# Storing the sample attention's mask and decays once, and repeating their rows while loading

## The chip, the core and the metric

One core of a Trainium2 chip runs the whole program. The metric is the device time of one execution, in microseconds; the time before is the median of three executions. Everything is float32. The engines named below are TensorE (PE in the profile, PEld its weight loads), VectorE (DVE), ScalarE (ACT), GpSimd (POOL) and SyncE (SP). SP, ACT and POOL issue DMA transfers, which the core's 16 DMA engines carry.

## What is computed

The reference is one inference step of a two-layer encoder trunk for two request groups with shared weights: a prompt group (1 x 256 tokens) and a sample group (8 requests x 16 new tokens, each with 512 cached keys, so 528 keys). A layer is SwiGLU, a token mixer, and SwiGLU again. The mixer has three attention branches of 6 heads x 64. What matters here is what is added to the scores of the sample group in two of them:

```python
def forgetting_attention(q, k, v, g_q, g_k, q_pos, k_pos):      # branch B
    s = einsum('bqhd,bkhd->bhqk', q, k) * scale
    s = s + g_kt[:, :, None, :] - g_q...        # decay: one row of keys per request and HEAD, the same for all tokens
    p = softmax(where(mask, s, -inf))

def dsa_attention(...):                          # branch C
    isc = ...                                    # indexer score per request, TOKEN and key, the same for all heads
    vals, idx = top_k(isc, topk)                 # the kernel keeps all keys and adds a mask of 0 or -1e30
    s = einsum(q, k_sel) * scale
    p = softmax(where(valid, s, -inf))
```

So the decays are 8 x 6 = 48 distinct rows of 528 numbers (g, without the query's own term, which a softmax does not need), and the mask is 8 x 16 = 128 distinct rows of 528.

## The kernel before, in words

The program is written out by hand, engine by engine, with semaphores; every engine runs its list in order. All work is in one function, `program`, with one block for each engine.

The sample attention of a layer runs in 18 steps (`NSTEP`), six for each branch: steps 0 to 5 stick-breaking, 6 to 11 forgetting, 12 to 17 DSA. A step (`UNIT = 4`) takes four pairs of heads: 4 pairs x 2 heads x 16 tokens fill the 128 partitions. Its scores are made by L1187 on PE into two banks; then L2328 on DVE scales them and adds the bias tile `BX[s % 2]`; DVE takes the maxima (L2341), ACT the exponentials (L1632), PE turns the probabilities one step later (L1158 and, for the new keys, L1164), multiplies them with the values (L1178), and forms the output two steps later (L1147). L2290 on DVE copies that output away, and stands behind L2328 in the DVE's list; L1164 on PE waits for it. PE also turns the keys of step s + 2 within step s (L1113). Eleven of the steps carry half a gate tile more (L1138); of steps 10 to 15 these are 11, 13 and 15.

Keys, values and bias stream from DRAM during the steps. `load_keys` (L572, SP) brings 768 KB for each request and branch into one of three buffers, as soon as PE has turned the keys that stood there. `load_values` and `load_new_values` (L1700, L1706, POOL) do so for the values with four buffers. `load_bias` (L1718, POOL) brings the bias of step s + 2 when L2328 of step s has read its buffer; there are two, `BX[0]` and `BX[1]`, both in the tile `MASKS`.

The bias comes from two scratch tensors in DRAM, `scr_g_sample` (`g_s`) and `scr_mask_sample` (`m_s`), each with a row for every request, head and token (768 x 528), so that a step's 128 rows lie in one piece. They are filled by SP:

- decays: `GX` (48 rows, in the tile QR) goes to `g_s` by one DMA (L539) that reads each row 16 times. This is during the projections, long before the steps.
- mask: DVE chooses the keys, in rounds between its other work, and ends in step 9 (`max(ROUND_S)`) with L2350, which writes the 128 rows of `WKS` (in the tile RING) as 0 or -1e30. SP then issues eight DMAs (L587), one for each request, each of which reads 16 rows 6 times. POOL waits for all eight (`msk_stored`) at the head of its step 10, and only then issues the bias of step 12, the first that reads `m_s`; the value loads of the DSA branch stand behind that wait in its list. On SP the remaining key loads of the DSA branch stand behind the eight stores.

Of the kernel before, what the change touches and what calls it, by code (L numbers as in the profile page):

```python
# [18 lines left out]
F32 = mybir.dt.float32  # L19

P = 128
# [3 lines left out]
NB = 8  # L25
NT = 16
# [5 lines left out]
KEYS = PAST + NT  # L32
PC = PAST // P
NH = 6
# [4 lines left out]
SB, FOX, DSA = range(NBR)  # L39
# [69 lines left out]
UNIT = 4  # L109
NU = NB * NPAIR // UNIT  # L110
# [27 lines left out]
def program(nc, t):  # L138
    with ExitStack() as ctx:
# [92 lines left out]
        WKS = RING[:, 7168 + MIX:7168 + MIX + KEYS]  # L232
# [40 lines left out]

        PS = ctx.enter_context(nc.psum_tensor("PS", [P, 8, 512], F32))

        g_s = nc.dram_tensor("scr_g_sample", (NB * NH * NT, KEYS), F32, kind="Internal").ap()
        g_p = nc.dram_tensor("scr_g_prompt", (NH, NPROMPT), F32, kind="Internal").ap()
        m_s = nc.dram_tensor("scr_mask_sample", (NB * NH * NT, KEYS), F32, kind="Internal").ap()


        def sems(name):
# [87 lines left out]
        def _(sp):  # L369
# [126 lines left out]
            for l in range(DEPTH):  # L496
# [5 lines left out]
                for i in range(N_PROJ):  # L502
# [33 lines left out]
                    if i == 9:  # L536
                        sp.wait_ge(g_ready, l * 2 + 2)
                        sp.dma_start(g_p, RSTD[0:NH, 0:NPROMPT]).then_inc(g_stored, 16)
                        sp.dma_start(g_s.rearrange("(g t) k -> g t k", t=NT),  # L539
                                     GX[0:48, :][:, None, :].to_broadcast([48, NT, KEYS])).then_inc(gs_stored, 16)  # L540

                def gates(g):
                    r = R_GATE + g - 1
# [34 lines left out]
                for s in range(-2, NSTEP):  # L578
                    for n in range(KBUF, NCACHE):
                        if last_unit(n - KBUF)[0] == s + 2:  # L580
                            load_keys(n)
                    if s == -1:
                        gates(7)
                    if s == max(ROUND_S):
                        sp.wait_ge(msk_ready, l * 3 + 3)
                        for b in range(NB):
                            sp.dma_start(m_s[b * NH * NT:(b + 1) * NH * NT, :].rearrange("(h t) k -> t h k", t=NT),  # L587
                                         WKS[b * NT:(b + 1) * NT, :][:, None, :].to_broadcast([NT, NH, KEYS])).then_inc(msk_stored, 16)

                w = t["w_branch"][l].rearrange("n (k p) d -> p (n k) d", p=P)  # L590
                for i in range(N_BRANCH):
                    r = R_BRANCH + i
                    if i < 2:
                        sp.wait_ge(gate_ready, l * 24 + 21 + 3 * i)
                        sp.wait_ge(msk_stored, (l + 1) * NB * 16)
                    else:
                        sp.wait_ge(br_ready, l * 24 + 6 * (i - 1))
                    load(l, r, by_k(l, r, w, i * 256, 256, k=9))
# [1095 lines left out]
        def _(pool):  # L1694
            for l in range(DEPTH):
# [12 lines left out]
                def load_bias(s):  # L1708

                    if s < NU + 2:  # L1710
                        pool.wait_ge(zs_ready, l * NSTEP + s + 1)
                    else:
                        pool.wait_ge(bx_free, l * 2 * NU + s - NU - 1)
                    if s == NU + 1:
                        pool.wait_ge(ps_ready, (l + 1) * NU)
                    settle(pool)
                    rows = (g_s, m_s)[s // NU - FOX]
                    pool.dma_start(BX[s % 2], rows[s % NU * P:(s % NU + 1) * P, :]).then_inc(bx_full[s % 2], 16)  # L1718

                pool.wait_ge(p_done, l * 6 + 2)  # L1720
                load_values(0)
# [8 lines left out]
                    load_new_values(n)  # L1730
                for s in range(NSTEP):
                    if s + 2 == 2 * NU:
                        pool.wait_ge(msk_stored, (l + 1) * NB * 16)
                        settle(pool)
                    if NU <= s + 2 < NSTEP:
                        load_bias(s + 2)
# [9 lines left out]
        def _(dve):  # L1746
# [328 lines left out]
            for l in range(DEPTH):  # L2075
# [242 lines left out]
                def step(s):  # L2318
# [4 lines left out]
                    begin()  # L2323
                    dve.wait_ge(ss_ready, l * NSTEP + s + 1)
                    if r != SB:
                        dve.wait_ge(bx_full[s % 2], l * (NU * 16) + ((s - NU) // 2 + 1) * 16)
                    bias = (ZERO[:, :] if r == SB else BX[s % 2]).rearrange("p (s k) -> p s k", s=2)
                    link(V.scalar_tensor_tensor(out=ZS.rearrange("p (s k) -> p s k", s=2), in0=PS[:, 4:6, 0:264],  # L2328
                                                scalar=SCALE, in1=bias, op0=ALU.mult, op1=ALU.add))
# [103 lines left out]
```

## Time and profile before

| | |
|---|---|
| median of 3 runs | 2439.22 us (2438.75 to 2440.55) |
| profiled execution, its own time | 2444.67 us |
| its span | 2442.9 us |
| PE busy | 2366.5 us, 97% of the span |
| DVE / ACT / POOL busy | 51% / 23% / 3% |
| granted TensorE clock, mean | 0.992 of full speed |
| DMA moved | 396.57 MB, 162 GB/s over the span |

The profile's page gives shares over the whole span; the timeline gives single instructions with start, duration and, in brackets, how long the engine had been idle and what ended that. A DMA instruction's duration in the timeline is its issue alone; how long the data took to land stands in the list of DMA issues. "Landing" below is counted from the start of the issue.

### The profile page before, as it was taken

To read this page: it belongs to the slowest core of one execution; us is meant where nothing else is said; L and a number is where in the kernel's file an instruction comes from. 1 tells how busy PE (TensorE), PEld (TensorE's weight loads), DVE (VectorE), ACT (ScalarE), POOL (GpSimd) and SP (SyncE) were. 2 spreads that over 40 slices of the span, in tenths; PEclk is the share of its full clock that TensorE was granted. 3 is DMA by queue.
4 is the path that set the end of the run, shared out by engine and by line. 5 is a ranking of instruction groups with operands and counts; after the bars stand their busy time and mean duration, and the time that the engine had idled before them with its cause. 6 is when DMAs were issued, how large, how long until landed. Compare 5 with 4: busy or idle time off the path is not lost.

```text
span 2442.9 us, 41219 instructions
## 1 busy us (share of the span) xinstructions
PE 2366.5 (97%) x17088; PEld 2044.6 (84%) x17088; DVE 1240.9 (51%) x2630; ACT 555.7 (23%) x1290; POOL 75.3 (3%) x124
## 2 busy tenths in 40 slices
PE   7999999999998999999999999999999989999998
PEld 6999996886665589999989999878756656999998
DVE  3656422534665426565265663235365844366742
ACT  3000022113553322001130000211235432410011
POOL 0000000000022000000000000000000220000000
PEclk9999999999999999999999999999999999999999
DMA  8354243773389342542325533447634883323232
GB/s 322 128 186 162 95 143 122 234 251 100 117 282 338 130 152 103 181 164 93 133 104 177 185 135 108 146 145 255 203 104 169 306 295 126 105 83 125 95 117 74
DMA packets 298634, 396.57 MB, mean 162 GB/s; under 512 B 31309, under 2 KB 243145, under 8 KB 298450
## 3 DMA queue, kind: packets, MB, share of 16 engines
q1 hardware_dynamic: 278690, 339.66, 41.3%
q0 software_dynamic: 12672, 45.42, 5.3%
q10 hardware_dynamic: 7088, 8.87, 1.0%
q8 instruction: 136, 2.23, 0.4%
q14 instruction: 48, 0.39, 0.0%
HBM read 378.54 MB, written 15.37 MB: 161 GB/s over the span
## 4 chain that ended last, share of the span: by engine, by line
PE 88%; DMA 4%; DVE 3%; SPq 2%; ACT 2%; issue 1%; DVEq 0%; ACTq 0%; POOLq 0%
PE PS L681 30%; PE PS L779 12%; PE PS L986 6%; PE PS L1228 4%; PE PS L934 4%; PE PS L880 3%; PE PS L651 2%; PE PS L827 2%; PE PS L835 2%; PE PS L956 2%; PE PS L720 2%; PE PS L1113 2%; DMA BIG<-w_ada 2%; PE PS L1138 2%; PE PS L1250 2%; PE PS L1242 2%
## 5 line engine op out<-in xcount | busy, mean ns | idle before, releaser
L681 PE MATMUL PS<-OT,RING 128*128 128x192 f32 x1280 | 234.2, 326 | 0.0
L681 PE MATMUL PS<-H,RING 128*128 128x192 f32 x1280 | 223.4, 328 | 0.0
L681 PE MATMUL PS<-OT,QR 128*128 128x192 f32 x1280 | 221.1, 326 | 0.0
L681 PEld LDWEIGHTS PS<-OT,RING 128*128 128x128 f32 x1280 | 212.4, 190 | 0.0
L681 PEld LDWEIGHTS PS<-H,RING 128*128 128x128 f32 x1280 | 208.4, 190 | 4.4 <-issue 4.1
L681 PEld LDWEIGHTS PS<-OT,QR 128*128 128x128 f32 x1280 | 210.2, 190 | 0.0
L1356 ACT ACTIVATE QR<-QR 128x384 f32<-128x384 f32 x80 | 41.8, 522 | 530.9 <-DVE QR L1916 530.9
L986 PE MATMUL PS<-H,RING 128*128 128x384 f32 x480 | 160.9, 490 | 0.0
L986 PEld LDWEIGHTS PS<-H,RING 128*128 128x128 f32 x480 | 89.1, 190 | 61.5 <-issue 4.7
L681 PE MATMUL PS<-H,QR 128*128 128x192 f32 x640 | 117.1, 326 | 0.0
L681 PEld LDWEIGHTS PS<-H,QR 128*128 128x128 f32 x640 | 106.2, 190 | 0.0
L1916 DVE TENSOR_TENSOR QR<-PS,QR 128x384 f32<-128x384 f32 x80 | 44.6, 557 | 110.7 <-PE PS L681 110.7
L1228 PE MATMUL PS<-OT,RING 128*128 128x384 f32 x288 | 93.4, 487 | 0.8 <-DVE OT L2290 0.8
L880 PE MATMUL PS<-RING,H 128*128 128x384 f32 (+1 forms) x288 | 90.9, 472 | 0.0
L779 PE MATMUL PS<-BIG,RING 128*128 128x192 f32 x528 | 89.7, 326 | 0.0
L1228 PEld LDWEIGHTS PS<-OT,RING 128*128 128x128 f32 x288 | 54.6, 190 | 38.7 <-DVE OT L2290 1.0
L779 PEld LDWEIGHTS PS<-BIG,RING 128*128 128x128 f32 x528 | 86.5, 190 | 0.0
L1968 DVE TENSOR_TENSOR QR<-RING 128x768 f32<-128x768 f32 (+1 forms) x24 | 21.3, 889 | 125.8 <-DMA RING<-ffn_w_out 125.8
L1911 DVE TENSOR_TENSOR QR<-PS,QR 128x384 f32<-128x384 f32 x80 | 44.4, 555 | 79.6 <-PE PS L681 79.4
L1113 PE MATMUL PS<-IDENT,QKT 128*128 128x128 f32 x576 | 77.7, 279 | 6.8 <-DMA QKT<-cache_dsa_k 4.2
L880 PEld LDWEIGHTS PS<-RING,H 128*128 128x128 f32 x288 | 54.0, 190 | 32.3 <-issue 1.4
L1113 PEld LDWEIGHTS PS<-IDENT,QKT 128*128 128x128 f32 x576 | 63.7, 142 | 17.0 <-issue 6.7
(308 smaller groups left out, 4043.7 us busy)
## 6 DMA issues: line engine op xcount, KB each, us to landing
RING<-ffn_w_in SPq DMA_DIRECT2D x80, 1024.0 KB, 7.2
RING<-w_in SPq DMA_DIRECT2D x64, 768.0 KB, 6.1
QR<-w_ada SPq DMA_DIRECT2D x34, 1024.0 KB, 9.7
BIG<-w_ada SPq DMA_DIRECT2D x34, 1024.0 KB, 10.3
RING<-ffn_w_out SPq DMA_DIRECT2D x32, 768.0 KB, 4.6
RING<-ffn_w_out SPq DMA_DIRECT2D x32, 640.0 KB, 5.3
QR<-cache_sb_v POOLq DMA_DIRECT2D x16, 768.0 KB, 5.9
QKT<-cache_sb_k SPq DMA_DIRECT2D x16, 768.0 KB, 6.4
```

Source lines behind the costliest of these rows:

```text
L651: mm = pe.matmul(PS[32 * j:32 * j + 32, bank, col:col + P], CT[:, k, :], w[:, k, j * P:(j + 1) * P], start=(k == 0), stop=(k == KD - 1))
L681: mm = pe.matmul(PS[:, bank, GROUP[g]], a[:, k, :], x[:, k, :], start=(k == 0), stop=(k == 3))
L720: mm = pe.matmul(PS[:, PLAIN_BANK[p] + part, GROUP[1]], w[:, k, part * 256 + jj * P:part * 256 + (jj + 1) * P], H[:, k, GROUP[1]], start=( ...
L779: mm = pe.matmul(PS[:, bank, 0:HALF], a[:, k, :], x[:, k, :], start=(half == 0 and k == 0), stop=(half == 1 and k == kn - 1))
L827: mm = pe.matmul(PS[:, m, 0:HALF], w[:, k, m * P:(m + 1) * P], HID[:, half * k2 + k, GROUP[0]], start=(half == 0 and k == 0), stop=(half = ...
L835: mm = pe.matmul(PS[:, m + 2, 0:HALF], w[:, k, m * P:(m + 1) * P], HID[:, half * k2 + k, GROUP[1]], start=(half == 0 and k == 0), stop=(ha ...
L880: mm = pe.matmul(PS[:, n % 3, 0:width], H[:, k, tt * P:(tt + 1) * P], w[:, k, :], start=(k == 0), stop=(k == KD - 1))
L934: mm = pe.matmul(PS[:, bank, GROUP[half]], a[:, k, :], x[:, k, :], start=(k == 0), stop=(k == 3))
L956: mm = pe.matmul(PS[:, 4, 0:MIX], H[:, k, 2 * P:T], w[:, k, :], start=(k == 0), stop=(k == KD - 1))
L986: mm = pe.matmul(PS[:, bank, 0:T], w[:, k, (n % 3) * P:(n % 3 + 1) * P], H[:, k, :], start=(k == 0), stop=(k == KD - 1))
L1113: mm = pe.transpose(PS[:, bank, c * P:(c + 1) * P], KC[:, n % KBUF, c, a * P:(a + 1) * P], IDENT[:, :])
L1228: mm = pe.matmul(PS[:, n, 0:T], w[:, 3 * n + k, m * P:(m + 1) * P], OT[:, 3 * n + k, :], start=(k == 0), stop=(k == NPAIR - 1))
```

## The change

The scratch tensors hold each distinct row once: `g_s` is 48 x 528 and `m_s` is 128 x 528. Each is written by one DMA without repeats. The repeating moves into `load_bias`: a decay load reads 8 rows of `g_s`, each 16 times (its source is a pattern of 8 x 16 x 528 with step 0 in the middle); a mask load is cut into the requests that the step touches, two for every step, and each part reads 16 rows of `m_s` 2, 4 or 6 times (a pattern of 2, 4 or 6 x 16 x 528 with step 0 outermost). The counts of the semaphores follow.

```diff
-        g_s = nc.dram_tensor("scr_g_sample", (NB * NH * NT, KEYS), F32, kind="Internal").ap()
+        g_s = nc.dram_tensor("scr_g_sample", (NB * NH, KEYS), F32, kind="Internal").ap()
-        m_s = nc.dram_tensor("scr_mask_sample", (NB * NH * NT, KEYS), F32, kind="Internal").ap()
+        m_s = nc.dram_tensor("scr_mask_sample", (NB * NT, KEYS), F32, kind="Internal").ap()
...
-                        sp.dma_start(g_s.rearrange("(g t) k -> g t k", t=NT),
-                                     GX[0:48, :][:, None, :].to_broadcast([48, NT, KEYS])).then_inc(gs_stored, 16)
+                        sp.dma_start(g_s, GX[0:48, :]).then_inc(gs_stored, 16)
...
-                        for b in range(NB):
-                            sp.dma_start(m_s[b * NH * NT:(b + 1) * NH * NT, :].rearrange("(h t) k -> t h k", t=NT),
-                                         WKS[b * NT:(b + 1) * NT, :][:, None, :].to_broadcast([NT, NH, KEYS])).then_inc(msk_stored, 16)
+                        sp.dma_start(m_s, WKS).then_inc(msk_stored, 16)
...
-                    rows = (g_s, m_s)[s // NU - FOX]
-                    pool.dma_start(BX[s % 2], rows[s % NU * P:(s % NU + 1) * P, :]).then_inc(bx_full[s % 2], 16)
+                    if s < 2 * NU:
+                        g = s % NU * 2 * UNIT
+                        pool.dma_start(BX[s % 2], g_s[g:g + 2 * UNIT, :][:, None, :].to_broadcast([2 * UNIT, NT, KEYS])).then_inc(bx_full[s % 2], 32)
+                    else:
+                        for i, j, b, a in unit_spans(s):
+                            pool.dma_start(BX[s % 2][2 * NT * i:2 * NT * j, :],
+                                           m_s[b * NT:(b + 1) * NT, :][None, :, :].to_broadcast([2 * (j - i), NT, KEYS])).then_inc(bx_full[s % 2], 16)
...
-                        dve.wait_ge(bx_full[s % 2], l * (NU * 16) + ((s - NU) // 2 + 1) * 16)
+                        dve.wait_ge(bx_full[s % 2], l * (NU * 32) + ((s - NU) // 2 + 1) * 32)
```

On SP, in the sample attention of the first layer, the list stands as follows, with the removed rows marked - and the new ones +. The names are the destination and, behind the arrow, the source, then the form written and how many such instructions follow each other.

```order
-L572 DMA QKT<-cache_sb_k 128x4x384 x3
-L572 DMA QKT<-cache_fox_k 128x4x384 x8
-L572 DMA QKT<-cache_dsa_k 128x4x384 x3
-L587 DMA scr_mask_sample<-RING 16x6x528 x8
-L572 DMA QKT<-cache_dsa_k 128x4x384 x5
+L571 DMA QKT<-cache_sb_k 128x4x384 x3
+L571 DMA QKT<-cache_fox_k 128x4x384 x8
+L571 DMA QKT<-cache_dsa_k 128x4x384 x3
+L585 DMA scr_mask_sample<-RING 128x528
+L571 DMA QKT<-cache_dsa_k 128x4x384 x5
```

The eight stores between the third and the fourth key load of the DSA branch have become one; nothing else on SP has moved (its lines only have other numbers).

On POOL, from the last loads of the forgetting branch into the DSA branch of the first layer, the list before is:

```order
L1718 DMA MASKS<-scr_mask_sample 128x528
L1700 DMA QR<-cache_dsa_v 128x4x384
L1706 DMA QR<-o_dsa_v_s 16x384
L1718 DMA MASKS<-scr_mask_sample 128x528
L1700 DMA QR<-cache_dsa_v 128x4x384
```

and after the change:

```order
L1719 DMA MASKS<-scr_mask_sample 96x1x528
L1719 DMA MASKS<-scr_mask_sample 32x1x528
L1697 DMA QR<-cache_dsa_v 128x4x384
L1703 DMA QR<-o_dsa_v_s 16x384
L1719 DMA MASKS<-scr_mask_sample 64x1x528 x2
L1697 DMA QR<-cache_dsa_v 128x4x384
```

Each mask load has become two (96 + 32, 64 + 64 or 32 + 96 partitions); their places among the value loads are the same. A decay load stays one instruction.

## Rows read from the trace of the kernel before

**Rows 1.** The page's first part: engine, busy us, share of span, instructions.

```profile
PE 2366.5 (97%) x17088; PEld 2044.6 (84%) x17088; DVE 1240.9 (51%) x2630; ACT 555.7 (23%) x1290; POOL 75.3 (3%) x124
```

**Rows 2.** Busy time by stretch: PE, PEld, DVE, ACT, POOL; PE clock, DMA share, GB/s.

```profile
720.00:740.00 20.00, 19.43 (x236) 13.60 (x236) 16.84 (x40) 10.38 (x16) 5.51 (x9) 1.00 0.94 323
770.00:780.00 10.00, 4.81 (x59) 3.47 (x58) 2.39 (x6) 2.42 (x4) 4.21 (x7) 0.78 0.98 344
```

**Rows 3.** Timeline of PE, layer 0, steps 10 to 15: start, duration, [idle before, releaser].

```profile
755.20 1.10 PE L1187 MATMUL PS<-QR,QBLK 128*32 128x264 f32 x16
...
756.94 1.47 PE L1113 MATMUL PS<-IDENT,QKT 128*128 128x128 f32 x12
...
760.93 1.10 PE L1187 MATMUL PS<-QR,QBLK 128*32 128x264 f32 x16
...
763.99 0.27 PE L1164 MATMUL PS<-IDENT,QR 128*16 128x128 f32 x1
...
768.72 1.10 PE L1187 MATMUL PS<-QR,QBLK 128*32 128x264 f32 x16
...
772.91 1.09 PE L1113 MATMUL PS<-IDENT,QKT 128*128 128x128 f32 x8 [1.84 <-DMA QKT<-cache_dsa_k]
...
776.86 0.38 PE L1164 MATMUL PS<-IDENT,QR 128*16 128x128 f32 x1 [2.85 <-DVE OT L2290]
...
781.22 1.68 PE L1187 MATMUL PS<-QR,QBLK 128*32 128x264 f32 x16
...
789.59 1.10 PE L1187 MATMUL PS<-QR,QBLK 128*32 128x264 f32 x16
...
793.12 0.65 PE L1113 MATMUL PS<-IDENT,QKT 128*128 128x128 f32 x4 [0.75 <-DMA QKT<-cache_dsa_k]
...
796.29 1.10 PE L1187 MATMUL PS<-QR,QBLK 128*32 128x264 f32 x16
```

**Rows 4.** Timeline of PE, layer 1, starts of steps 12, 13 and 14.

```profile
1969.99 1.10 PE L1187 MATMUL PS<-QR,QBLK 128*32 128x264 f32 x16
...
1982.22 1.92 PE L1187 MATMUL PS<-QR,QBLK 128*32 128x264 f32 x16
...
1990.83 1.10 PE L1187 MATMUL PS<-QR,QBLK 128*32 128x264 f32 x16
```

**Rows 5.** Timeline of SP, DVE and POOL, layer 0, from the stores to step 12.

```profile
755.78 4.69 SPq L587 DMA_DIRECT2D scr_mask_sample<-RING  x8
...
760.58 21.17 SPq L572 DMA_DIRECT2D QKT<-cache_dsa_k  x4
...
762.10 0.71 DVE L2328 SCALAR_TENSOR_TENSOR DMB<-PS,MASKS 128x528 f32<-128x528 f32 x1 [1.06 <-PE PS L1187]
...
770.31 0.56 POOL L1718 DMA_DIRECT2D MASKS<-scr_mask_sample  x1 [12.42 <-DMA scr_mask_sample<-RING]
...
775.66 0.71 DVE L2328 SCALAR_TENSOR_TENSOR DMB<-PS,MASKS 128x528 f32<-128x528 f32 x1 [6.84 <-DMA MASKS<-scr_mask_sample]
```

**Rows 6.** DMA issues of layer 0, single ones: KB, us to landing.

```profile
scr_mask_sample<-RING SPq DMA_DIRECT2D x1, 198.0 KB, 6.9
...
QKT<-cache_dsa_k SPq DMA_DIRECT2D x1, 768.0 KB, 12.3
...
MASKS<-scr_mask_sample POOLq DMA_DIRECT2D x1, 264.0 KB, 5.2
...
MASKS<-scr_mask_sample POOLq DMA_DIRECT2D x1, 264.0 KB, 8.9
...
QR<-cache_dsa_v POOLq DMA_DIRECT2D x1, 768.0 KB, 7.1
```

**Rows 7.** DMA issues: the prompt's decays, 6 KB read by all 128 partitions.

```profile
QR<-scr_g_prompt SPq DMA_DIRECT2D x1, 768.0 KB, 4.1
```

**Rows 8.** The decays' store, layer 0: landing, and PE's next work after it.

```profile
scr_g_sample<-QR SPq DMA_DIRECT2D x1, 1584.0 KB, 16.8
...
532.44 1.95 PE L651 MATMUL PS<-BIG,CT 128*32 128x128 f32 x64
```

More of the change, by code:

```diff
@@ L594, in _ @@
                         sp.wait_ge(gate_ready, l * 24 + 21 + 3 * i)
-                        sp.wait_ge(msk_stored, (l + 1) * NB * 16)
+                        sp.wait_ge(msk_stored, (l + 1) * 16)
                     else:
@@ L1732, in _ @@
                     if s + 2 == 2 * NU:
-                        pool.wait_ge(msk_stored, (l + 1) * NB * 16)
+                        pool.wait_ge(msk_stored, (l + 1) * 16)
                         settle(pool)
```

## Prediction

> **What bounds the kernel now.** The page's first part comes first: PE is busy for 97% of the span [rows 1], so an edit to transfers can only pay where PE waits for one. Next are the stretches. While the forgetting branch runs, PE is busy for 19.43 of 20 us, with the DMA engines at 0.94 of their time and 323 GB/s. In the ten microseconds after 770 it is busy for 4.81, the granted clock is 0.78, and the DMA engines are at 0.98 [rows 2]. The timeline of PE says what a step costs: from one L1187 to the next it is 760.93 - 755.20 = 5.73 us without a gate half (step 10) and 768.72 - 760.93 = 7.79 us with one (step 11). Against these, layer 0 spends
>
> - step 12: 781.22 - 768.72 = 12.50, an excess of 6.77
> - step 13: 789.59 - 781.22 = 8.37, an excess of 0.58
> - step 14: 796.29 - 789.59 = 6.70, an excess of 0.97, of which 0.75 is a wait for keys
>
> together 8.32 us [rows 3]. Layer 1 has 1982.22 - 1969.99 = 12.23 and 1990.83 - 1982.22 = 8.61, an excess of 6.50 + 0.82 = 7.32 [rows 4]. So 15.64 us of the span lie in this one place, and nothing else that the change touches has PE waiting.
>
> What ends the waits there: in step 12 L2328 starts at 775.66, after 6.84 us of waiting for the mask, while the scores would have let it start 1.17 after L1187 (as in step 11: 762.10 - 760.93), at 769.89. It is 5.77 late. L1164 on PE waits behind it, until 776.86; undisturbed it comes 3.06 after L1187 (763.99 - 760.93), at 771.78, and L1164 needs L2328 to start 776.86 - 775.66 = 1.20 before it. So L2328 may start at 770.58 without anybody noticing: 0.69 of slack, and 5.08 of the 5.77 reach PE. The remaining 1.7 of step 12 and most of step 13 is PE at a lower clock after it has stood idle: L1187 takes 1.68 in place of 1.10 [rows 3, 5]. Under the same roof stands a second wait: L1113 waits until 772.91 for the keys that were issued at 760.58 and landed after 12.3 us [rows 3, 5, 6]. It hides behind the mask now, and would be next: 1.84 us.
>
> **The mask's store.** Before: eight issues take 4.69 us of SP from 755.78, and POOL gets through its wait only at 770.31 [rows 5]. They carry 8 x 198 = 1584 KB. After: one issue of 264 KB at the same 755.78, since the mask is ready when it was. The first of the eight landed after 6.9 us [rows 6], behind the same older transfers; 66 KB more at the 344 GB/s of rows 2 is 0.2. Landed at 762.9, and with 0.6 for POOL to see it and start, the first load of step 12's mask starts at about 763.5, 6.8 us before today's 770.31. In 1320 KB less there are also 3.9 us of all 16 DMA engines, in a stretch in which they are full.
>
> **The mask's loads.** Two instructions instead of one: 0.56 us of POOL more for each of six steps and two layers, 6.7 us on an engine that is busy for 3% [rows 1]. In step 12 that is on the path: the second part starts at 764.06. Today's load of the same step lands after 5.2 [rows 6]. What a load of a repeated source costs, the trace doesn't show for this pattern; the bounds are these. From below, no more than today, or less: the prompt's decays, 6 KB read again for each of 128 partitions, bring 768 KB in 4.1 us [rows 7], so a repeated source is in itself no hot spot. From above: if a load whose source has 8, 6, 4 or 2 blocks is carried by only as many DMA engines, each of them carries 16 rows, 33.8 KB, where sixteen carried 8 rows each. 16.9 KB more on an engine that moves 344/16 = 21.5 GB/s is 0.8 us, and twice that if other queues take every other turn; and a value load, with 48 KB on each engine, landed after 7.1 in the same crowd [rows 6], which is the upper end. I take 5.2 + 0.8 = 6.0, nearer to the row of the same step: landed at 770.1, L2328 starts at 770.2, within the slack of 770.58. With the upper end it starts at 771.3, 0.7 too late. As the estimate lies so close to the edge, I leave 0.6 for each layer.
>
> The row for the prompt's decays shows 768 KB landing at full spread, at 4.1 us [rows 7]. Against taking that for the new loads speaks the Trainium skill, DMA: Bandwidth & Descriptors, section "Why a DMA increments its semaphore by 16 and not by 1": the number of DMA engines is the largest up to 16 that divides the slowest dimension of both patterns, so 8 for the decays and 6, 4 or 2 for the parts of the mask, where the prompt's pattern has 128 in front. No row of this case shows a load of such a form. By that rule the 0.8 us above is owed (the sum stands as it is), without it nothing is, and the 0.6 for each layer goes: 2423.6.
>
> **The other steps.** The bias of step s + 2 is asked for when L2328 of step s is through, and needed two steps later: 5.73 + 7.79 = 13.5 us. The longest landing of a mask today is 8.9 [rows 6]; with 1.6 for the doubled share and 0.6 for the second issue it is 11.1. It stays hidden by the other 2.4. The same holds for the decays, which land no later in a forgetting branch that PE crosses at 19.43 of 20 us [rows 2].
>
> **Keys and values behind it.** SP is free at about 756.3. The next key load then waits only for its buffer, which L1113 of step 10 gives back at 756.94 + 1.47 = 758.41 [rows 3]. It goes at about 758.5 instead of 760.58, with 1320 KB fewer in front of it: even with the old 12.3 it lands at 770.8, and PE wants it at about 771.0. Less the 3.9 us of traffic it lands at 767. That wait of 1.84 goes too. The value loads that now stand behind POOL's wait of 12.42 [rows 5] move some 6 us forward, which spreads the crowd. The DSA branch then looks like the forgetting branch, which has the same keys, values and bias in each step and no wait of PE for any of them.
>
> **The decays' store.** 1584 KB that took 16.8 us to land become 99 KB. PE goes on at 532.44 without an idle bracket, in the middle of it [rows 8], and the steps that read them are 180 us away. Worth nothing; if a weight load beside it should come earlier, PE still has no wait there to lose.
>
> **The sum.** 8.32 + 7.32 = 15.6, less 2 x 0.6, is 14.4 us. The profiled execution took 2444.67, 5.5 over the median; its span of 2442.9 becomes 2428.5, and the median 2439.22 becomes 2424.8.
>
> **The rivals.**
>
> *The loads are thin (few engines).* The mechanism above at its upper end, with a store that is slow too. The last of the eight stores was issued at about 760.0 and seen at about 769.7, 9.7 us later [rows 5]; midway between that and the first's 6.9 is 8.3, 1.2 more than assumed, and the load takes 7.1 rather than 6.0, 1.1 more. L2328 starts at 772.5, 1.9 too late, and some of the low clock stays: 3 us in each layer, together 6. Gain 9.6: 2429.6. For it: DMA engines at 0.98; against it: the crowd itself gets 1320 KB smaller. The Trainium skill's rule on the number of engines, cited above, is what would bring it about, and no row contradicts it. Chance 0.2.
>
> *The keys become the bound.* Four requests of 768 KB keys and 768 KB values in three steps, and 264 KB of bias in each, are 2312 KB in (5.73 + 7.79)/2 = 6.76 us, 350 GB/s, no less than the 344 of rows 2; and what the mask gave back is asked for earlier. The wait of 0.75 in step 14 stays and the one of 1.84 stays: 2.6 in each layer, 5.2 together. Gain 10.4: 2428.8. Against it: the forgetting branch runs at 323 GB/s without such waits [rows 2]. Chance 0.08.
>
> *Slower.* Each of the 24 bias loads lands late. The place is L2328 in steps 6 to 17, the price 1 us for each two steps and each us of landing over 12.2 (13.5 less issue and L2328), that is 12 us over both layers. It outweighs the gain of 14.4 from a landing of 13.4 on; at 16 us, three times today's, it costs 46, and 2439.2 - 14.4 + 46 is 2471. That needs a source of 8 or 16 rows to be read much slower than one of 6 KB, against [rows 7], or an extra cost of POOL's making of the pattern. Chance 0.06.
>
> *No change.* The mask wait goes but another as long ends in its place (the store of 128 rows is no faster than eight of 96 side by side, and the stall stays within 5 us). Against it: 6.9 us for the first of the eight [rows 6]. Chance 0.05: 2437.
>
> **How the numbers follow.** Forecast 0.61: 2424.8, with its own range 2422 to 2427 (all 15.6 and a little, or 1.7 of late mask in each layer). The range reaches into the two cases beside it, 2421.5 to 2431.5; outside lie slower, no change and the tail of thin loads. The measurement tells 0.2%, about 4.9 us, from no change. Faster 0.88, same 0.06, slower 0.06.
>
> **What the changed profile would show.** One L585 issue in place of 4.69 us of eight; POOL's first mask load of the DSA branch at about 8 us after that issue, where it is 14.5 now; L2328 of step 12 with at most 1 us of wait for MASKS; L1187 of steps 12, 13 and 14 at 5.7 to 6.5, 7.8 and 5.7 us from each other; clock 1.00 there. Landings of the decay and mask loads of 5 to 8 us. The prediction is wrong if these landings pass 9, if POOL's wait still ends over 10 us after the store's issue, or if PE's steps 6 to 11 grow.

## The result and the profile after

The changed kernel is slower: 2450.70 us (median of 5 runs, 2449.92 to 2451.59) beside 2439.22 (5 runs); the ratio is 1.0046, with a 95% interval of 1.0035 to 1.0057. The forecast was 2424.8, with a range of 2421.5 to 2431.5. Ratios and intervals, here and below, leave out single executions that ran far longer than the rest (one of 2766.6 us at a granted clock of 0.85 among those of the last kernel below, and one of 7185 us of the kernel before).

In its profiled execution (2451.4 us, span 2449.6) the lines that are L1187, L1113, L1164, L2328 and L587 before are L1184, L1110, L1161, L2330 and L585. The page's first part and its queue of POOL's transfers, which answer to [rows 1]:

```profile
PE 2366.3 (97%) x17088; PEld 2043.2 (83%) x17088; DVE 1240.8 (51%) x2630; ACT 555.8 (23%) x1290; POOL 85.2 (3%) x136
...
q0 software_dynamic: 15936, 45.45, 5.9%
```

PE does the same work in the same 2366 us, so the time is in waits. The waits of PE for transfers of keys (the view of waits: engine, tile, line, releaser: us in total, times, longest):

```profile
PE PS L1110 <- DMA QKT<-cache_dsa_k: 9.9, 3, 5.0
...
PE PS L1110 <- DMA QKT<-cache_fox_k: 5.1, 4, 1.9
```

Before, the forgetting branch (`fox`) had no such line. The timeline of PE shows where, in layer 0 (answers to [rows 3]):

```profile
740.76 0.66 PE L1110 MATMUL PS<-IDENT,QKT 128*128 128x128 f32 x4 [1.88 <-DMA QKT<-cache_fox_k]
...
749.16 1.09 PE L1110 MATMUL PS<-IDENT,QKT 128*128 128x128 f32 x8 [1.48 <-DMA QKT<-cache_fox_k]
...
768.35 1.10 PE L1184 MATMUL PS<-QR,QBLK 128*32 128x264 f32 x16
...
774.04 0.28 PE L1161 MATMUL PS<-IDENT,QR 128*16 128x128 f32 x1 [2.48 <-DVE OT L2292]
...
778.39 1.10 PE L1184 MATMUL PS<-QR,QBLK 128*32 128x264 f32 x16
...
786.18 1.10 PE L1184 MATMUL PS<-QR,QBLK 128*32 128x264 f32 x16
...
793.59 1.12 PE L1110 MATMUL PS<-IDENT,QKT 128*128 128x128 f32 x4 [4.63 <-DMA QKT<-cache_dsa_k]
...
798.87 1.10 PE L1184 MATMUL PS<-QR,QBLK 128*32 128x264 f32 x16
```

Step 12 still costs 778.39 - 768.35 = 10.04 us (12.50 before), step 13 has its undisturbed 7.79, and step 14, 6.70 before, is 12.69. What belongs to the mask, on POOL, DVE and SP (answers to [rows 5]):

```profile
755.41 0.50 SPq L585 DMA_DIRECT2D scr_mask_sample<-RING  x1
...
758.13 23.93 SPq L571 DMA_DIRECT2D QKT<-cache_dsa_k  x5
...
767.63 0.62 POOL L1719 DMA_DIRECT2D MASKS<-scr_mask_sample  x1 [10.11 <-DMA scr_mask_sample<-RING]
...
772.85 0.71 DVE L2330 SCALAR_TENSOR_TENSOR DMB<-PS,MASKS 128x528 f32<-128x528 f32 x1 [4.39 <-DMA MASKS<-scr_mask_sample]
```

One store, as meant, and POOL gets through its wait 12.2 us after the store's issue, where it was 14.5. In layer 1 the wait for the mask (2.85 us) is the only other one that L2330 has for a bias; step 12 costs 6.97 there, where it was 12.23, and step 14 costs 13.07, where it was 5.74:

```profile
1997.58 1.11 PE L1110 MATMUL PS<-IDENT,QKT 128*128 128x128 f32 x4 [5.00 <-DMA QKT<-cache_dsa_k]
```

So where most of the mask's stall was won, more than that was lost again at the keys. The store's 16 completions, one for each part of the transfer, as the trace has them in layer 0 (us):

```
15 of 16: 761.74 ... 762.50
the last: 766.84
```

And the landings, from the list of DMA issues: of the whole program first, then single ones of layer 0 (a decay load and a key load of the forgetting branch, issued within 3 us of each other after 730; a key load and the two parts of a mask load issued after 781):

```profile
MASKS<-scr_g_sample POOLq DMA_DIRECT2D x12, 264.0 KB, 8.8
MASKS<-scr_mask_sample POOLq DMA_DIRECT2D x8, 198.0 KB, 6.7
MASKS<-scr_mask_sample POOLq DMA_DIRECT2D x8, 132.0 KB, 8.6
MASKS<-scr_mask_sample POOLq DMA_DIRECT2D x8, 66.0 KB, 6.2
...
QKT<-cache_fox_k SPq DMA_DIRECT2D x1, 768.0 KB, 17.5
MASKS<-scr_g_sample POOLq DMA_DIRECT2D x1, 264.0 KB, 13.3
...
QKT<-cache_dsa_k SPq DMA_DIRECT2D x1, 768.0 KB, 18.6
MASKS<-scr_mask_sample POOLq DMA_DIRECT2D x1, 198.0 KB, 11.6
MASKS<-scr_mask_sample POOLq DMA_DIRECT2D x1, 66.0 KB, 12.7
```

The median of the decay loads was 4.9 before; the one of 13.3 has as its counterpart one of 8.7, the key load of 17.5 one of 9.5, and that of 18.6 one of 10.2. The key load that PE waits for at 793.59 is the one before the last: issued at 778.55, it took 15.0. In the pair issued after 781, the 66 KB part of the mask takes as long as that of 198. The same stretches of the changed kernel as in [rows 2] (busy time of PE, PEld, DVE, ACT, POOL; clock, DMA share, GB/s):

```profile
720.00:740.00 20.00, 18.32 (x242) 12.45 (x240) 15.54 (x39) 8.19 (x13) 7.65 (x12) 1.00 1.00 310
770.00:780.00 10.00, 6.93 (x81) 4.82 (x80) 3.35 (x9) 3.02 (x5) 6.24 (x10) 0.83 0.98 265
```

The whole stretch from 716 to 756, first before, then after the change:

```profile
716.00:756.00 40.00, 37.50 (x482) 25.35 (x480) 33.70 (x81) 17.88 (x29) 11.12 (x18) 1.00 0.94 323
```

```profile
716.00:756.00 40.00, 34.25 (x419) 23.16 (x417) 29.78 (x74) 16.79 (x27) 10.61 (x17) 1.00 0.99 288
```

So the DMA engines (at a share near or over 1 they have no time left) are busier and bring less: 288 GB/s at a share of 0.99, where it was 323 at 0.94. From 764 to 796 before has 351 GB/s at 1.00 (34 of them are mask stores that the change no longer has), after 280 at 0.98.

A tally over both layers shows where the result lies. The undisturbed step costs 5.73 or 7.79 us in the DSA branch (steps 12 to 15; 4.60 from step 16 to 17), and in the other two branches what it costs before; what a step takes above that is its excess. The kernels below the second row are the experiments that follow.

| kernel | median us | excess, steps 0 to 11 | excess, steps 12 to 16 | sum | median less sum |
|---|---|---|---|---|---|
| before | 2439.2 | 0.0 | 15.6 | 15.6 | 2423.6 |
| after | 2450.7 | 6.0 | 20.6 | 26.5 | 2424.2 |
| decays once | 2446.6 | 4.6 | 16.9 | 21.5 | 2425.1 |
| mask once | 2442.4 | 0.1 | 16.5 | 16.6 | 2425.8 |
| decays twice, 16 blocks | 2440.7 | 1.2 | 13.8 | 15.0 | 2425.7 |
| all rows, read in 8 blocks | 2444.7 | 6.8 | 13.1 | 19.8 | 2424.9 |
| all rows, read in 4 blocks | 2452.0 | 10.2 | 14.8 | 25.0 | 2427.0 |
| before, stores spread | 2436.4 | 0.0 | 12.9 | 12.9 | 2423.5 |
| before, wait in parts | 2437.7 | 0.0 | 12.2 | 12.2 | 2425.5 |
| mask once, eight loads | 2431.1 | 0.1 | 8.9 | 9.0 | 2422.1 |
| the same, decays twice | 2433.3 | 5.4 | 7.2 | 12.5 | 2420.8 |
| mask twice, four loads | 2439.5 | 0.0 | 14.0 | 14.1 | 2425.4 |
| mask once, four thin loads | 2441.4 | 0.0 | 15.5 | 15.5 | 2425.9 |

The excess is from one profiled execution of each, the median from five or more, so the last column is constant only to about 3 us either way. The first two sums differ by 10.9 us, the medians by 11.5. The two profiled executions themselves differ by less, 6.7 us: that of before took 5.5 over its median, and its steps begin late, at 681.62 in layer 0 where after has 677.44. So the tally says where the waits are, and the medians how much time they cost; differences of under 3 us between two rows are not to be read from it.

### The profile page after: what moved, and what is told of

Same layout as the page of the kernel before. It is cut to its first block, busy times and chain, and to the rows that moved or that the text cites. A ratio compares the mean times of both kernels' runs of the same rounds, so it can differ in the third digit from the quotient of the medians.

```text
span 2449.6 us, 41217 instructions
## 1 busy us (share of the span) xinstructions
PE 2366.3 (97%) x17088; PEld 2043.2 (83%) x17088; DVE 1240.8 (51%) x2630; ACT 555.8 (23%) x1290; POOL 85.2 (3%) x136
## 4 chain that ended last, share of the span: by engine, by line
PE 86%; DMA 6%; DVE 3%; ACT 2%; SPq 2%; issue 1%; DVEq 0%; POOL 0%; ACTq 0%; POOLq 0%
PE PS L678 29%; PE PS L776 12%; PE PS L983 6%; PE PS L1225 4%; PE PS L931 4%; PE PS L877 3%; PE PS L648 2%; PE PS L824 2%; PE PS L832 2%; PE PS L953 2%; PE PS L717 2%; DMA BIG<-w_ada 2%; PE PS L1247 2%; PE PS L1239 2%; PE PS L1110 2%; PE PS L1135 1%
## 5 line engine op out<-in xcount | busy, mean ns | idle before, releaser
L1110 PE MATMUL PS<-IDENT,QKT 128*128 128x128 f32 x576 | 79.7, 282 | 17.6 <-DMA QKT<-cache_dsa_k 9.9
L1110 PEld LDWEIGHTS PS<-IDENT,QKT 128*128 128x128 f32 x576 | 64.6, 143 | 28.7 <-DMA QKT<-cache_dsa_k 10.1
## 6 DMA issues: line engine op xcount, KB each, us to landing
BIG<-w_ada SPq DMA_DIRECT2D x34, 1024.0 KB, 10.2
```

The lines of the kernel that those rows point to most:

```text
L1110: mm = pe.transpose(PS[:, bank, c * P:(c + 1) * P], KC[:, n % KBUF, c, a * P:(a + 1) * P], IDENT[:, :])
```

## The experiments

Every kernel computes the whole output. In each the lines of the sample attention are a few numbers off those of before: the turning of the keys is L1110 to L1116, the adding of the bias L2328 to L2337, the bias load L1716 to L1722. The kernel before was timed again beside each group: 2439.6 beside the first four experiments (decays once to 8 blocks), 2440.0 beside the 4 blocks and the two kernels with four mask loads, 2440.4 beside the other four. A ratio is against the kernel before of its own group, so a difference of two ratios is safer than one of two medians of the table.

The outer blocks of a load are the entries of the outermost dimension of its source pattern: 8 for the decays of the change, 2 to 6 for its mask's parts. A load with fewer than 16 is called thin here, one with 16 or more wide. Theory A: a thin load costs more DMA time, and the keys, which share the DMA engines, pay. Theory B: reading the same rows again and again is slow. Theory C: the mask's new path (one store, two issues on POOL) is what costs.

**Each half alone.** Decays once, mask as before:

```diff
-g_s = dram (NB * NH * NT, KEYS)
+g_s = dram (NB * NH, KEYS)
...
-pool.dma_start(BX[s % 2], g_s[s % NU * P:(s % NU + 1) * P, :])
+pool.dma_start(BX[s % 2], g_s[s % NU * 8:s % NU * 8 + 8, :][:, None, :].to_broadcast([8, NT, KEYS]))
```

> Only the decays are changed: 48 rows are stored, a load reads 8 rows 16 times each; mask stored and loaded as before. Few-engines theory (a load whose source pattern has 8 outer blocks is carried by 8 of the 16 DMA engines) and slow-repeats theory (reading one row again and again is slow) both expect the decay loads to land after some 9 us instead of 4.9, steps 8 and 9 of the sample attention to take 2 and 1.7 us more in layer 0 and 1.2 and 1.0 in layer 1, and the kernel to come out about 5 us slower than before, near 2444. If instead the loss is all in the masks, this run equals the kernel before within 2 us.

Mask once, decays as before (the diff is the mask's part of the change):

> Only the masks are changed: 128 rows stored by one DMA, each step's mask loaded in two parts of 2, 4 or 6 outer blocks; decays as before. Expected: step 12 shorter than before by more than the 2.5 and 5.3 us it gained in the full change, since the mask's store no longer lands in the wake of thin decay loads; step 14 about 6 us longer (a wait for keys). Time between -2 and +6 us against before. If the two parts of the change add up, d1 and d2 together give the +11.5 of the full change.

Measured: decays once 2446.60, ratio 1.0022 (1.0013 to 1.0031); mask once 2442.38, 1.0007 (0.9998 to 1.0016). Both shares together are 0.29%, of the 0.46% of the change. The 0.17% between them is no wider than its own interval, so that the two halves also hurt each other is likely (the tally has 5.9 and 1.0 us more than before, against 10.9), not shown. The decay loads land after 8.4 us (median) with the decays once, near the 9 that were expected; the steps that grow are 8 in both layers and 11 in layer 1, not 8 and 9. With the decays once alone, PE waits for the keys of the forgetting branch in both layers, while its mask path is untouched:

```profile
740.64 0.66 PE L1112 MATMUL PS<-IDENT,QKT 128*128 128x128 f32 x4 [0.94 <-DMA QKT<-cache_fox_k]
...
1946.90 0.66 PE L1112 MATMUL PS<-IDENT,QKT 128*128 128x128 f32 x4 [1.48 <-DMA QKT<-cache_fox_k]
```

With the mask once alone, the store's 16 completions come within 0.6 us of each other in layer 0, and the store lands after 7.1 us (7.3 in layer 1), as forecast; step 12 costs 7.03 in layer 0, and the mask wait of 6.84 is down to 2.91. What was won comes back one and two steps later, at the keys:

```profile
769.24 0.71 DVE L2330 SCALAR_TENSOR_TENSOR DMB<-PS,MASKS 128x528 f32<-128x528 f32 x1 [2.91 <-DMA MASKS<-scr_mask_sample]
...
782.59 0.63 PE L1111 MATMUL PS<-IDENT,QKT 128*128 128x128 f32 x4 [2.06 <-DMA QKT<-cache_dsa_k]
...
789.16 0.66 PE L1111 MATMUL PS<-IDENT,QKT 128*128 128x128 f32 x4 [1.62 <-DMA QKT<-cache_dsa_k]
...
1989.25 1.11 PE L1111 MATMUL PS<-IDENT,QKT 128*128 128x128 f32 x4 [4.33 <-DMA QKT<-cache_dsa_k]
```

So the mask's part alone costs nothing that the measurement tells, and wins nothing. Against theory C stands above all a kernel further down: it has the same single store and more issues on POOL, and is faster than before. The store's straggling completion (766.84) is absent here. Of the other kernels with a single store one more has a straggler, by 2.3 us, in layer 0 of the kernel with eight mask loads and the decays twice, which has no thin load; no run shows the cause.

**Repeats or blocks.** The next two keep everything but the decay loads as before. Before, a load's outermost dimension is its 128 rows. One kernel stores each decay row twice and reads 16 blocks of one row, 8 times each: repeated reads, but 16 blocks.

```diff
-g_s[s % NU * P:(s % NU + 1) * P, :]
+g_s[s % NU * 16:s % NU * 16 + 16, :][:, None, :].to_broadcast([16, 8, KEYS])
```

> Decays only: each distinct row stored twice (96 rows), a load reads 16 rows 8 times each, so the source pattern has 16 outer blocks. Few-engines theory: all 16 engines carry it, landings of 4 to 6 us, steps 8 and 9 as before (5.7 and 9.2 us), time as before within 1 us. Slow-repeats theory: 8 of 16 readings are still repeats, landings of 8 to 9 us, steps 8 and 9 longer, about 4 us slower. If a pattern of three levels as such is the cause (more and smaller packets), it behaves as the slow-repeats theory says, and the packets of POOL's queue rise as in the full change (by 136 for a load).

The other kernel stores all 768 rows with an empty row behind each 16, and reads 8 blocks of 16 distinct rows: no repeats, but 8 blocks.

```diff
-g_s[s % NU * P:(s % NU + 1) * P, :]
+g_s[s % NU * 136:(s % NU + 1) * 136, :].rearrange("(g t) k -> g t k", t=17)[:, 0:NT, :]
```

> Decays only: all 16 copies of each row are stored as before, with one unused row after each group of 16, so that a load's source is a pattern of 8 blocks of 16 different rows; no row is read twice. Few-engines theory: as slow as d1, landings near 9 us, about 5 us over before. Slow-repeats theory: as before, landings near 5 us. Three-levels theory: as d1.

Measured: 16 blocks with repeats 2440.71, ratio 1.0005 (0.9997 to 1.0014), landing 7.5; 8 blocks without repeats 2444.69, 1.0020 (1.0011 to 1.0028), landing 8.7:

```profile
MASKS<-scr_g_sample POOLq DMA_DIRECT2D x12, 264.0 KB, 7.5
```

```profile
MASKS<-scr_g_sample POOLq DMA_DIRECT2D x12, 264.0 KB, 8.7
```

Theory B alone would have the two the other way round. It has a small part: with the repeats at 16 blocks the landing is 7.5 against 4.9 (few engines alone had let expect 4 to 6, slow repeats 8 to 9), and there is one key wait of 0.95 in the forgetting branch, but the time can't be told from before's.

**A larger dose.** The same 768 distinct rows, an empty row behind each 32, in 4 blocks:

```diff
+g_s[s % NU * 132:(s % NU + 1) * 132, :].rearrange("(g t) k -> g t k", t=33)[:, 0:2 * NT, :]
```

> The decays are stored as before, all 768 rows (by two stores, with one empty row behind each 32), and each decay load reads 4 blocks of 32 distinct rows, 66 KB each; nothing is repeated, the mask is as before. Theory (a load is carried by as many DMA engines as its source has blocks, and the keys that share these engines pay): 4 engines carry 66 KB each where 8 carried 33, so the landing goes from the 8.7 of the 8-block run to 11 to 14 us, the waits of PE for fox_k from 3.2 to 5 to 9 us together, and the time from 2444.7 to 2448 to 2456. Rival (what costs is the gap in the source or the added small packets, not the number of engines): landing and time as with 8 blocks, 2443 to 2446.

Measured: 2452.03, ratio 1.0059 (1.0045 to 1.0072). Landing 10.0 (11 to 14 expected), waits for the keys of the forgetting branch 6.0 us (5 to 9 expected). An outermost dimension of 128, 8 and 4, with the same distinct rows, gives 2439.2, 2444.7 and 2452.0: 5.5 us more, and then another 7.3. The gap in the source is there with 8 and with 4 blocks (even rarer with 4), so the gap as the cause falls; the small packets are priced below. In the stretch from 716 to 756 the DMA engines bring 275 GB/s at a share of 1.04:

```profile
716.00:756.00 40.00, 34.92 (x409) 23.90 (x402) 29.56 (x72) 16.20 (x27) 10.80 (x17) 0.96 1.04 275
```

The packets of that stretch, counted in the trace by their size, show where the DMA time goes:

| 716 to 756 us | 8-byte packets | key packet, 1536 bytes | bias packet, 4224 bytes |
|---|---|---|---|
| before, 128 rows in one piece | 0 | 72 ns | 211 ns |
| 16 blocks, repeated | 0 | 78 ns | 232 ns |
| 8 blocks | 384 | 83 ns | 238 ns |
| after, 8 blocks, repeated | 323 | 87 ns | 259 ns |
| 4 blocks | 980 | 95 ns | 264 ns |

Loads of few blocks come with extra packets of 8 bytes. At 10 to 11 ns each they are 980 x 11 = 11 us of the 640 us that 16 engines have there, 1.7%, and 0.5% after the change: not the cost. What grows is the mean time of the key packets, which nobody has changed, from 72 to 87 ns (after) and to 95 ns (4 blocks); in the other kernels that leave the decays as before it is 72 to 75. It is a part of them that is slowed: the median is 65 to 66 ns in the first four rows of the table and 91 with 4 blocks, while the share of key packets that take over 100 ns goes from 3% to 16% (8 blocks), 22% (after) and 33% (4 blocks); with 16 repeated blocks it is 9%, with the decays once alone 20% (median 71). There the loss appears, and the keys are its victim.

The traces also show how many of the bias's packets of 4224 bytes are under way at once, from 690 to 760 us, as a share of the time in which any is:

| 690 to 760 us | more than 4 | more than 8 |
|---|---|---|
| before, 128 rows in one piece | 48% | 36% |
| 16 blocks, repeated | 36% | 23% |
| 8 blocks | 39% | 1% |
| after, 8 blocks, repeated | 35% | 1% |
| 4 blocks | 4% | 0% |

The count stops at the number of blocks, with distinct rows and with repeated ones alike. That fits one DMA engine for each block; the trace does not name a packet's engine.

**Where the gain went.** Two kernels leave the data and the loads as before and only bring the mask forward. In the first, the eight stores are issued in three lots (2, 2 and 4, in steps 9, 10 and 11), with a semaphore for each lot, so that POOL can start step 12's load after two of them:

```diff
+if max(ROUND_S) <= s <= max(ROUND_S) + 2:
+    for b in ((0, 1), (2, 3), (4, 5, 6, 7))[s - max(ROUND_S)]:
...
+                 .then_inc((msk_a, msk_b, msk_stored, msk_stored)[b // 2], 16)
```

> The kernel before (all 768 mask rows stored, wide loads), but the eight stores are issued in three lots: requests 0 and 1 in step 9, 2 and 3 after the key load of step 10, 4 to 7 after that of step 11, each lot with its own semaphore, and POOL waits for a lot only before the load that reads it. If the stall of step 12 is the latency of the store that its load waits for plus keys held up behind the other stores, step 12 falls from 12.5 to about 6 us in both layers and the kernel gains 12 to 15 us: 2425 to 2428. If the DMA engines are short of time in the DSA branch whatever the order, the gain stays under 6 us, and the keys' waits grow.

The second issues all eight at once, as before, and only POOL's wait is cut into the same three parts:

```diff
 if s + 2 == 2 * NU:
-    pool.wait_ge(msk_stored, (l + 1) * NB * 16)
+    pool.wait_ge(msk_a, (l + 1) * 32)
...
+if s + 2 == 2 * NU + 1:
+    pool.wait_ge(msk_b, (l + 1) * 32)
...
+if s + 2 == 2 * NU + 3:
+    pool.wait_ge(msk_stored, (l + 1) * 64)
```

> The kernel before with all eight stores where they are, but POOL waits before the load of step 12 for the first two stores alone, before step 13's for the next two, before step 15's for the rest. It keeps the 1584 KB in front of the keys. Expected: L2328 of step 12 no longer waits; the wait for keys of 1.84 us stays; step 12 at 7.5 to 8, gain 8 to 10 us: 2430.

Measured: stores spread 2436.38, ratio 0.9984 (0.9975 to 0.9993); in parts 2437.74, 0.9992 (0.9982 to 1.0001). Both fall far short of the 12 to 15 and the 8 to 10 us that were expected; the first has what its other branch named, a gain under 6 us. The second can't be told from no gain. With the wait in parts:

```profile
763.28 0.56 POOL L1720 DMA_DIRECT2D MASKS<-scr_mask_sample  x1 [8.06 <-DMA scr_mask_sample<-RING]
...
770.87 1.09 PE L1115 MATMUL PS<-IDENT,QKT 128*128 128x128 f32 x8 [2.48 <-DMA QKT<-cache_dsa_k]
...
771.68 0.71 DVE L2336 SCALAR_TENSOR_TENSOR DMB<-PS,MASKS 128x528 f32<-128x528 f32 x1 [5.53 <-DMA MASKS<-scr_mask_sample]
```

The load follows its wait 4.4 us sooner than in [rows 5] (8.06 against 12.42), but from its issue to L2336 it now takes 771.68 - 763.28 = 8.40 us, where it was 775.66 - 770.31 = 5.35: it flies among the stores. DVE's wait is 1.3 us shorter (5.53 against 6.84), and step 12 is shorter by the same 1.3 us (1.8 in layer 1). With the stores spread, DVE still waits 3.76 and 4.00 us for the mask, and PE 4.8 us for the keys. Here, where all the data come over full DMA engines, the wait isn't undone by asking earlier; neither kernel has a thin load, and neither came near the 14.4 us of the forecast.

**A mask load that is wide.** The mask stored once, as in the change, but each step's bias brought by eight loads of 16 distinct rows (33 KB), decays as before:

```diff
-for i, j, b, a in unit_spans(s):
-    pool.dma_start(BX[s % 2][2 * NT * i:2 * NT * j, :],
-                   m_s[b * NT:(b + 1) * NT, :][None, :, :].to_broadcast([2 * (j - i), NT, KEYS]))
+for q in range(2 * UNIT):
+    b = unit_groups(s)[q // 2][0] % NB
+    pool.dma_start(BX[s % 2][NT * q:NT * (q + 1), :], m_s[b * NT:(b + 1) * NT, :])
```

> The mask stored once (128 rows, one DMA), as in the changed kernel, but each step's mask is loaded by eight DMAs of 16 rows, whose patterns have 16 in front on both sides; decays as before. Few-engines theory: with every load on all 16 engines the gain that was forecast for the change appears: step 12 at 5.7 to 7, step 14 at 5.7, 12 to 15 us faster than before. If repeated reading or the later value loads cause the stall of step 14, it stays (12 us there) and the time is that of d2, within 3 us of before. Eight issues take about 4.4 us of POOL in each of these steps, so value loads may go out 3 us later than in d2.

And the same with the decays stored twice, in 16 repeated blocks:

> f2's mask and d3's decays (each row stored twice, 16 blocks read 8 times). Few-engines theory: the two parts add up, so f2's time within 1.5 us: 2425 to 2428. Slow-repeats theory: slower than f2 by 3 us or more, in steps 8 and 9.

Measured: 2431.13, ratio 0.9968 (0.9957 to 0.9979), the best of this study, but 8 us below before and not the 12 to 15 that were expected; with the decays twice 2433.34, 0.9972 (0.9963 to 0.9981). Against the same store with two thin loads (2442.4, ratio 1.0007) the eight loads are some 10 us faster, though POOL issues for 3.82 us where it was 1.24. The lists of DMA issues and of waits of the eight-load kernel:

```profile
MASKS<-scr_mask_sample POOLq DMA_DIRECT2D x96, 33.0 KB, 5.9
...
QKT<-cache_dsa_k SPq DMA_DIRECT2D x16, 768.0 KB, 8.0
...
PE PS L1111 <- DMA QKT<-cache_dsa_k: 3.3, 1, 3.3
```

The keys land after 8.0 us (median) where it was 10.2 with the mask's two thin loads, and PE waits for them for 3.3 us rather than 8.0. Step 12 keeps a mask wait (3.37 in layer 0), since the mask is still chosen, stored and read back over busy DMA engines, and step 14 of layer 1 still costs 10.16.

With the decays twice the time was expected within 1.5 us of the eight loads alone if only the blocks count, and 3 or more above if repeats are slow; the 2.2 us lie between and can't be told from none (0.9968 and 0.9972). But its trace has waits of 3.2 us for the keys of the forgetting branch and 5.4 us of excess in steps 0 to 11, from decay loads that land after 8.0 us. So 16 repeated blocks are cheaper than 8, and not free.

**The same number of loads, thin and wide.** With four loads of 66 KB for each step: once of 32 distinct rows (the mask stored twice, by eight stores of 66 KB), once of 16 rows read twice, so 2 blocks (the mask stored once):

```diff
+for q in range(UNIT):
+    b = unit_groups(s)[q][0] % NB
+    pool.dma_start(BX[s % 2][2 * NT * q:2 * NT * (q + 1), :], m_s[b * 2 * NT:(b + 1) * 2 * NT, :])
```

```diff
+for q in range(UNIT):
+    b = unit_groups(s)[q][0] % NB
+    pool.dma_start(BX[s % 2][2 * NT * q:2 * NT * (q + 1), :],
+                   m_s[b * NT:(b + 1) * NT, :][None, :, :].to_broadcast([2, NT, KEYS]))
```

> Decays as before. The mask is stored twice for each token (8 stores of 66 KB, 528 KB together), so that a step's mask comes by four loads of 32 distinct rows, 66 KB each, on all 16 DMA engines. Theory (wide loads are cheap, POOL's issues cost little): POOL needs 1.9 us for the four where eight took 3.8, the stores' last landing at 8 to 9 us after the first issue where one store took 6.3; the two balance, 2430 to 2434, beside 2431.1 for eight loads. Rival (it is the small store alone that gave the 8 us of the eight-load version): 528 KB and eight issues give back half, 2434 to 2437.

> Decays as before, mask stored once by one store of 264 KB. A step's mask comes by four loads as in the version with two copies, but each reads 16 rows twice (a pattern of 2 x 16 x 528). Theory (2 blocks are carried by 2 DMA engines, 33.8 KB on each; four such loads on the same two engines would be 135 KB there): landings of 9 to 14 us, waits for dsa_k and the mask of over 15 us together, 2443 to 2460, slower than before. Rival (the number of loads or the store decides, not the blocks): no slower than the version with two copies, 2428 to 2434.

Measured: wide 2439.51, ratio 0.9999 (0.9990 to 1.0008); thin 2441.44, 1.0002 (0.9993 to 1.0012). Both expectations were missed: the wide one gains nothing over before, and the thin one, put at 2443 to 2460, can't be told from the wide one. In the landings the difference is there, first wide, then thin:

```profile
MASKS<-scr_mask_sample POOLq DMA_DIRECT2D x48, 66.0 KB, 5.7
...
scr_mask_sample<-RING SPq DMA_DIRECT2D x16, 66.0 KB, 5.8
```

```profile
MASKS<-scr_mask_sample POOLq DMA_DIRECT2D x48, 66.0 KB, 7.8
...
scr_mask_sample<-RING SPq DMA_DIRECT2D x2, 264.0 KB, 7.1
```

and in the stretch from 764 to 796 the DMA engines bring 311 GB/s at 0.99 with the wide loads, 290 at 1.07 with the thin ones. But the wide version pays for eight stores: POOL waits for 9.77 us, against 5.90. The cleaner pair is the same single store with eight wide loads (2431.1, ratio 0.9968) and with four thin ones (2441.4, 1.0002), some 8 to 10 us, though these differ in the number of loads too. That the loads of 2 blocks all go to the same two DMA engines, as was assumed for the expectation, is not so: of the time in which mask packets are under way from 764 to 812, 28% has 5 to 8 of them at once (and under 1% more than 8; with the four wide loads 29%). What makes four wide loads (2439.5) so much worse than eight (2431.1) is settled only in part: POOL's wait for the stores is 3.9 us longer in layer 0 and 6.0 in layer 1, DVE's waits for the mask come to 10.5 us against 7.2, and the remaining 5 us stay open.

## Why the prediction was wrong

**Bottleneck.** Right: 15.6 us of stall in steps 12 to 14 of the two layers, behind the mask; and the tally above follows the medians over thirteen kernels.

**The mask's store.** Forecast to land 7.1 us after its issue. 15 of its 16 completions were there after 7.1, the last after 11.4, and POOL went on after 12.2, not 7.7. In layer 1 the store landed after 7.9, and with the mask alone changed after 7.2. The first of the eight stores [rows 6] gave the right size; it couldn't show that one part in sixteen might be held up.

**The mask's loads.** Forecast 6.0 for step 12; in layer 0 the two parts took 2.7 and 4.2, better. In layer 1 they took 5.0 and 5.2. The price of a thin load was taken as its own longer landing, against the slack of the one instruction that reads it. This is the step that failed. L2330 waited for its bias in step 12 alone, in both layers; the cost of the other 22 loads fell on the keys. Of the 25.9 us between forecast and result, 6.0 are the excess in steps 0 to 11, put at nothing, and 19.4 are in steps 12 to 16, where a gain of 14.4 was forecast and the excess grew by 5.0.

**"It stays hidden ... The same holds for the decays."** The landing was bounded at 11.1 for the mask and put at no more than today's for the decays; 13.3 occurred for a decay load and 12.7 and, in layer 1, 14.4 for parts of a mask, and the median of the decays went from 4.9 to 8.8. The bias itself stayed hidden even so. But the DMA engines were at 0.94 to 0.98 of their time [rows 2], and the work on them grew: from 72 to 87 ns for the mean key packet. A key load then took 17.5 us, where its counterpart had taken 9.5, and PE waited. The forgetting branch, where the forecast had nothing, lost 6.0 us. A stretch at 0.94 has no room for transfers that become 10 or 20% dearer, and that number stood in [rows 2].

The Trainium skill, DMA: Bandwidth & Descriptors, section "Why a DMA increments its semaphore by 16 and not by 1", has the number of DMA engines depend on the slowest dimension, and was cited in the prediction with an effect of 0.8 us for each load. The runs bear out that this dimension matters (128, 8 and 4: 2439.2, 2444.7, 2452.0), and the traces agree with the number: more than 8 packets of the bias are under way at once for 36% of the time before and for 1% with 8 blocks. That each load then costs no more than its own longer landing was the prediction's addition, and wrong.

**Keys and values.** The first key load behind the store went 2.7 us after it, as forecast, and landed after 10.8 us, in time: right, and the wait of 1.84 is gone. The later ones came into a worse crowd, and the waits of 4.63 and 5.00 in step 14 took its place. "The DSA branch then looks like the forgetting branch" fell even without thin loads: with the stores spread the branch keeps 12.9 us of excess, with four wide loads 14.0. The rival "the keys become the bound" had worked out 350 GB/s of need against 344, priced it at 5.2 us and was given 0.08; with the stores spread PE waits for keys for 4.8 us, with the mask once for 8.0.

**The rivals.** Few engines had the right cause, but priced at L2328. Slower had the right sign, but at the same wrong place and with a threshold (landings over 13.4) that no bias load passed in layer 0; in layer 1 one passed it (14.4), and L2330 did not wait for it. Neither asked who else uses the engines.

**The decays' store.** Worth nothing, right: it lands after 9.7 instead of 16.8 us in layer 0, and nobody waits.

## What to carry to other kernels

Where the DMA engines are at 0.9 of their time or more, price a change of a transfer's form by what it does to all others in the same stretch, by DMA share and GB/s together, and look for the victim in the largest transfer with the least slack. Let the outermost dimension of a small load have 16 or more entries: eight loads of 16 distinct rows were some 10 us better here than two that repeat rows in 2 to 6 blocks, in spite of 2.6 us more of issuing for each step, though four wide loads with eight stores won nothing over before. And a stall on data over full DMA engines is not worth its length: the best version here is 8 us faster where 15.6 were lost.

## What the runs showed of the hardware

- A load's number of outer blocks changes the time of packets of other queues: the key packets of 1536 bytes take 72 ns in the mean beside bias loads of 128 rows in one piece, 83 with 8 blocks, 95 with 4. It is a part of them that is slowed (3%, 16% and 33% take over 100 ns).
- Of a load with k outer blocks no more than about k packets of data are under way at once: more than 8 for 36% of the time before and 1% with 8 blocks, more than 4 for 4% with 4 blocks. Loads of few blocks that follow each other still use different engines: with four loads of 2 blocks for each step, 5 to 8 packets are under way for 28% of the time.
- Loads of few blocks bring packets of 8 bytes with them, 64 for each load of 8 blocks and 192 for each of 4 (page: 13440 and 14976 packets on POOL's queue, 12672 before, for 12 loads), and 112 for each 32-row load of 2 blocks (18624 packets for 48 such loads, of which 576 of the 5952 more are of 4 bytes). For each packet of 4224 bytes that is 1 with 8 blocks, 3 with 4 and 7 with 2; with 16 blocks there are none. They take 10 to 13 ns each.
- A thin load's landing doesn't go with its size: 198, 132 and 66 KB took 6.7, 8.6 and 6.2 us (medians; they belong to different steps), and in one step 11.6 for 198 and 12.7 for 66.
- Of the 16 completions of one store, 15 can be there 4.3 us before the last. Only their times show it; the list of DMA issues has 11.4 us for the whole.
- 128 rows read as 16 blocks with each row repeated 8 times land after 7.5 us, as distinct rows in one piece after 4.9, though the time of the kernel is the same within what is measured.
